# Products of activations and gates shared with GpSimd, loads by pairs and by eight, and another order at the end of a decoder layer with a PEER mixer

## The reference, cut to what matters

```python
    best, pos = lax.top_k(cand, K)
    expert_idx = jnp.take_along_axis(cand_idx, pos, axis=-1)
    gate = jax.nn.softmax(best, axis=-1)
    ...
        u = jnp.take(expert_down, idx, axis=0)
        a = jax.nn.gelu(jnp.einsum('nd,nhkd->nhk', xb, u).astype(jnp.float32), approximate=False)
        w = (gb * a).astype(xb.dtype)
        v = jnp.take(expert_up, idx, axis=0)
        return jnp.einsum('nhk,nhkd->nd', w, v)
    ...
    return rmsnorm(x, final_norm_w)
```

## Time and profile before

| | us |
|---|---|
| three runs | 1594.74, 1594.9, 1597.07 |
| median | 1594.9 |
| the profiled execution, its own time | 1598.4 |
| its span, first to last instruction | 1596.2 |
| mean granted TensorE clock | 0.997 of full speed |
| busy in the span: PE, DVE, ACT, POOL | 1568.7, 1167.0, 665.1, 977.4 |
| first instruction of block 1 of the second product | at 1084.51 |

### The profile page before, as it was taken

How to read it: one execution, slowest core, us unless ns; L and a number is a source line. 1 busy time by engine, 2 the same in 40 slices (tenths; PEclk the granted TensorE clock), 3 DMA queues, 4 the chain that set the end, 5 groups by cost and what they waited for, 6 DMA issues and landing times.

```text
span 1596.2 us, 26546 instructions
## 1 busy us (share of the span) xinstructions
PE 1568.7 (98%) x9939; PEld 1481.5 (93%) x9939; DVE 1167.0 (73%) x2248; ACT 665.1 (42%) x991; POOL 977.4 (61%) x563
## 2 busy tenths in 40 slices
PE   8999999999999999999999999999999999999997
PEld 6888888888989999999999999999999999999997
DVE  4155361342479999999999973348999999998996
ACT  5352442542434444444444443333343333333334
POOL 4463376523235899887777778875566465675632
PEclk9999999999999999999999999999999999999998
DMA  4232243313423999989999999969999999999991
GB/s 185 93 102 70 70 155 93 112 61 106 158 80 120 293 355 345 327 291 314 372 391 408 394 413 391 348 212 381 402 400 402 400 402 392 400 402 384 402 373 74
DMA packets 158768, 441.80 MB, mean 277 GB/s; under 512 B 16208, under 2 KB 66384, under 8 KB 158544
## 3 DMA queue, kind: packets, MB, share of 16 engines
q1 hardware_dynamic: 88656, 228.88, 40.6%
q0 software_dynamic: 46080, 167.79, 27.6%
q10 hardware_dynamic: 23936, 43.85, 7.2%
HBM read 396.65 MB, written 43.25 MB: 276 GB/s over the span
## 4 chain that ended last, share of the span: by engine, by line
PE 63%; DMA 15%; DVE 9%; issue 6%; ACT 2%; POOL 2%; SPq 1%; ACTq 0%; DVEq 0%
PE psum L1512 18%; PE psum L1513 18%; PE psum L1514 18%; DMA arena<-up_in 7%; DMA arena<-hid_dram 5%; PE psum L1799 4%; DVE kept L1401 3%; DVE arena L1415 2%; POOL w_low L460 2%; DVE wgt_low L1426 1%; DMA gate_dram<-arena 1%; PE psum L1748 1%; PE psum L1776 1%; DMA kept<-up_in,arena 1%; SPq L371 1%
## 5 line engine op out<-in xcount | busy, mean ns | idle before, releaser
L460 POOL TENSOR_TENSOR w_low<-kept,w_high 128x1024 fp32r<-128x1024 f32 x212 | 520.0, 2456 | 310.9 <-ACT w_high L589 309.1
L1512 PE MATMUL psum<-hT_high,w_high 128*128 128x352 f32 (+2 forms) x1408 | 484.6, 344 | 4.1 <-POOL w_low L460 3.4
L1514 PE MATMUL psum<-hT_high,w_low 128*128 128x352 f32 (+2 forms) x1408 | 476.7, 339 | 0.0
L1513 PE MATMUL psum<-hT_low,w_high 128*128 128x352 f32 (+2 forms) x1408 | 476.7, 339 | 0.0
L1512 PE MATMUL psum<-wgt_high,up_high 128*128 128x352 f32 x1016 | 329.7, 324 | 4.5 <-DVE wgt_low L1426 4.5
L1514 PE MATMUL psum<-wgt_high,up_low 128*128 128x352 f32 x1016 | 328.0, 323 | 0.0
L1513 PE MATMUL psum<-wgt_low,up_high 128*128 128x352 f32 x1016 | 327.8, 323 | 0.0
L1512 PEld LDWEIGHTS psum<-hT_high,w_high 128*128 128x128 f32 x1408 | 264.8, 188 | 18.6 <-POOL w_low L460 2.6
L589 ACT ACTIVATE w_high<-kept 128x1024 fp32r<-128x1024 f32 x212 | 223.5, 1056 | 134.1 <-PE psum L1514 90.8
L1514 PEld LDWEIGHTS psum<-hT_high,w_low 128*128 128x128 f32 x1408 | 264.7, 188 | 12.7
L1513 PEld LDWEIGHTS psum<-hT_low,w_high 128*128 128x128 f32 x1408 | 265.0, 188 | 12.0 <-issue 0.5
(11 more groups left out here) (277 smaller groups left out, 2047.9 us busy)
## 6 DMA issues: line engine op xcount, KB each, us to landing
kept<-down_in SPq DMA_DIRECT2D x128, 512.0 KB, 6.8
arena<-up_in SPq DMA_DIRECT2D x128, 512.0 KB, 13.8
kept<-front_w SPq DMA_DIRECT2D x92, 512.0 KB, 3.6
gate_dram<-arena ACTq DMA_DIRECT2D x40, 512.0 KB, 9.3
arena<-hid_dram SPq DMA_DIRECT2D x112, 176.0 KB, 12.8
kept<-gate_dram SPq DMA_DIRECT2D x24, 640.0 KB, 16.5
hid_dram<-arena ACTq DMA_DIRECT2D x56, 176.0 KB, 6.8
hid_dram<-kept ACTq DMA_DIRECT2D x56, 176.0 KB
```

The costliest lines, as they stand in the source:

```text
L460: nc.gpsimd.tensor_tensor(lower, ring[:, p % RING, :], high.bitcast(F32), ALU.subtract).then_inc(low_ready, 1)
L1512: nc.tensor.matmul(out, lhs[0], rhs[0], start=first, stop=False)
L1513: nc.tensor.matmul(out, lhs[0], rhs[1], start=False, stop=False)
L1514: return nc.tensor.matmul(out, lhs[1], rhs[0], start=False, stop=last)
```

## The change

- Activations go out and come in by pairs of blocks (352 KB): two pair buffers out (`PAIRS_OUT`), four in (`PAIRS_IN`, so eight blocks). The pair of blocks u, u + 1 is asked for when block u - 7 is weighed; the wait for DVE in SP's queue is there for every second block only.
- Gates are stored and loaded by groups of eight blocks (1280 KB), two buffers; a load of gates has 10 KB in a row for each partition, a piece of a store two rows of 2 KB. `PIECES_AT` stores a chunk's pieces by step 5 instead of step 6. The first load of gates no longer waits for the last dot.
- The 32-column product moves from DVE to POOL (`weigh_near`), with a semaphore `near_ready` that ACT's `weight_high` and SP's `load_hid` wait for. In POOL's program it stands among the gathers.
- At the end: sums of squares in parts of 512, 256 and 256 columns, tiles 0 and 1 on ACT and tile 2 on DVE; the last 256 columns of the product with the gain on DVE; the scaling and the stores in halves; PE turns bank o - 1 back behind bank o.
- Some buffers move.

```diff
-GT = 4
+GT = 8
+GROUPS = NK // GT
 PIECES = 8
-PIECES_AT = (1, 1, 1, 1, 1, 1, 2, 0)
+PIECES_AT = (2, 1, 1, 1, 2, 1, 0, 0)
...
-HIDS = 4
+PAIRS_OUT, PAIRS_IN = 2, 4
...
-        gates = [at(kb, FAR * GT * CH, FAR, GT * CH) for kb in (116, 45, 50, 55)]
-        hidr = at(60, 4 * DN, 4, DN)
+        gates = [at(kb, FAR * GT * CH, FAR, GT * CH) for kb in (192, 45)]
+        hidr = at(60, 2 * PAIRS_IN * DE, 2 * PAIRS_IN, DE)
...
-            def load_gates(i, s):
-
-                sp.dma_start(gates[s], gate_dram[:, :, bass.ds(i * CH, GT * CH)]).then_inc(ld_gate[s], 16)
-
-            def load_hid(i, s):
-                sp.dma_start(hidr[:, s, 0:DE], hid_dram[bass.ds(i, 1)].rearrange("b p n -> (b p) n")).then_inc(ld_hid[s], 16)
+            def load_gates(g, s):
+
+                sp.dma_start(gates[s], gate_dram[:, bass.ds(g, 1)].rearrange("p g c n -> p (g c) n")).then_inc(ld_gate[s], 16)
+
+            def load_hid(j, s):
+                sp.dma_start(hidr[:, 2 * s:2 * s + 2, :].rearrange("p a n -> p (a n)"),
+                             hid_dram[bass.ds(j, 1)].rearrange("b p n -> (b p) n")).then_inc(ld_hid[s], 16)
...
-                    sp.wait_ge(dot_done, ROWS)
-                    load_gates(block_of(0), 0)
+                    load_gates(SPILL // GT, 0)
...
-            def next_block(u, i, s, quad=True):
-
-                sp.wait_ge(w_raw, u * 2 - 6)
-                load_hid(i, s % 4)
+                if u % GT == GT // 2:
+                    sp.wait_ge(w_raw, u + GT // 2 - GT)
+                    load_gates((u + GT // 2 - KEEP) // GT, (u // GT + 1) % 2)
+
+            def next_block(u, i, pair, group, s, quad=True):
+
+                if s % 2 == 0:
+                    sp.wait_ge(w_raw, u - 6)
+                    sp.wait_ge(near_ready, u - 6)
+                    load_hid(pair, s // 2 % PAIRS_IN)
                 sp.wait_ge(up_done, u + 1 - RING_U)
                 load_up(i, s % RING_U)
-                if s % 4 == 0 and quad:
-                    load_gates(i + GT, (s // 4 + 1) % 4)
+                if s % GT == GT // 2 and quad:
+                    sp.wait_ge(w_raw, u - GT // 2)
+                    load_gates(group, (s // GT + 1) % 2)
...
+            def weigh_near(u):
+                if u < KEEP:
+                    pool.wait_ge(gelu_out, SPILL + u + 3)
+                    h = hid_kept[u]
+                else:
+                    pool.wait_ge(ld_hid[u // 2 % PAIRS_IN], 16 * ((u - KEEP) // 2 // PAIRS_IN + 1))
+                    h = hidr[:, u % (2 * PAIRS_IN), :]
+                if u >= 4:
+                    pool.wait_ge(w_ready, u - 3)
+                nc.gpsimd.tensor_tensor(wraw[:, u % 4, FAR * CH:DE], h[:, FAR * CH:DE], near[:, (u + SPILL) % NK, :], ALU.mult)\
+                    .then_inc(near_ready, 1)
+
             for i in range(AHEAD + 2, NK):
+                if i == NK - 3:
+                    pool.wait_ge(gate_out, 2 * STEPS + 3)
+                    weigh_near(0)
+                    weigh_near(1)
...
+            weighed = 2
             up_rows = up_in.rearrange("b p n -> (b p) n")
             for k in range(UP_ROWS):
                 if k < UP_FIRST:
                     pool.wait_ge(block_used, USED + NK - UP_FIRST + k + 1)
                 elif k == UP_FIRST:
                     pool.wait_ge(block_used, USED + NK)
+                    pool.wait_ge(dot_done, ROWS)
                 if UP_FIRST <= k < RING_C:
                     pool.wait_ge(up_done, k - UP_FIRST + 1)
                 if UP_FIRST + 2 <= k < RING_C:
-                    pool.wait_ge(w_raw, 2 * (3 if k == UP_FIRST + 2 else 6))
+                    pool.wait_ge(w_raw, 3 if k == UP_FIRST + 2 else 6)
+                    pool.wait_ge(near_ready, 3 if k == UP_FIRST + 2 else 6)
                 if k >= RING_C:
                     pool.wait_ge(sparse_added, k - RING_C + 1)
                 numbers = edge_idx[:, k:k + 1] if k < EDGE_SLOTS else idx3[:, k - EDGE_SLOTS:k - EDGE_SLOTS + 1]
                 nc.gpsimd.indirect_dma_start(rows_c[k % RING_C], None, up_rows,
                                              bass.IndirectOffsetOnAxis(numbers.bitcast(U32), 0))\
                     .then_inc(ld_c[k % RING_C], 16)
+                while weighed < min(NK, (k - RING_C) * (NK - 4) // UP_ROWS + 4 if k >= RING_C else k):
+                    weigh_near(weighed)
+                    weighed += 1
+            while weighed < NK:
+                weigh_near(weighed)
+                weighed += 1
 
             pool.wait_ge(ld_fin, 16)
-            for o in range(KC):
+            for o in range(KC - 2):
...
             def weight_high(i, s):
-                act.wait_ge(w_raw, i * 2 + 2)
+                act.wait_ge(w_raw, i + 1)
+                act.wait_ge(near_ready, i + 1)
...
-                if i >= HIDS:
-                    act.wait_ge(hid_stored[i % HIDS], 16 * (i // HIDS))
-                nc.scalar.activation(hid[i % HIDS], psum[:, 4 + i % 2, 0:DE], ACT.Gelu).then_inc(gelu_out, 1)
-                act.wait_ge(gelu_out, i + 3)
-                act.dma_start(hid_dram[i], hid[i % HIDS]).then_inc(hid_stored[i % HIDS], 16)
+                j, half = i // 2, i % 2
+                if half == 0 and j >= PAIRS_OUT:
+                    act.wait_ge(hid_stored[j % PAIRS_OUT], 16 * (j // PAIRS_OUT))
+                nc.scalar.activation(hid[j % PAIRS_OUT][:, half, :], psum[:, 4 + i % 2, 0:DE], ACT.Gelu).then_inc(gelu_out, 1)
+                if half:
+                    act.wait_ge(gelu_out, i + 3)
+                    act.dma_start(hid_dram[j], hid[j % PAIRS_OUT].rearrange("p a n -> p (a n)"))\
+                        .then_inc(hid_stored[j % PAIRS_OUT], 16)
...
-                act.dma_start(gate_dram[:, c, q * rows * CH:(q + 1) * rows * CH],
-                              stage[:, c % 2, q * rows:(q + 1) * rows, :].rearrange("p i n -> p (i n)"))\
+                act.dma_start(gate_dram[:, q * rows // GT:(q + 1) * rows // GT, c, :],
+                              stage[:, c % 2, q * rows:(q + 1) * rows, :].rearrange("p (g b) n -> p g (b n)", b=GT))\
...
-                    t = o - 5
                     act.wait_ge(x_added, 4)
-                    step.put(nc.scalar.activation(junk[:, 0:512], x[:, t, 0:512], ACT.Square, accum_out=ss[:, t:t + 1]))
                     step.end()
+                    square(o - 5, FIRST_COLS, ss)
+            act.wait_ge(x_added, 6)
+            for t in range(2):
+                step.end()
+                square(t, MORE_COLS, ss[:, NT:])
             act.wait_ge(x_added, KC)
+            for t in range(2):
+                step.end()
+                square(t, LAST_COLS, ss[:, 2 * NT:])
             step.end()
-            nc.scalar.activation(junk[:, 512:D], x[:, 0, 512:D], ACT.Square, accum_out=ss[:, NT:NT + 1]).then_inc(fin_squares, 1)
+            act.sem_inc(fin_squares, 1)
...
+            for c in (slice(0, 512), slice(512, D)):
+                step(nc.scalar.activation(fin_out[:, 1, c], fin_out[:, 1, c], ACT.Copy, scale=rs[:, 1:2]))
+                act.dma_start(out[P:2 * P, c], fin_out[:, 1, c]).then_inc(out_stored, 16)
...
-            def weigh(i, s, quad, gate_landed, landed, block, kept_hid=None):
-                dve.wait_ge(ld_gate[quad], gate_landed)
+            def weigh(i, landed, block, kept_hid=None):
+                s = i % 4
+                dve.wait_ge(ld_gate[i // GT % 2], 16 * (i // GT // 2 + 1))
                 if kept_hid is None:
-                    dve.wait_ge(ld_hid[s % 4], landed)
+                    dve.wait_ge(ld_hid[i // 2 % PAIRS_IN], 16 * ((i - KEEP) // 2 // PAIRS_IN + 1))
                 else:
                     dve.wait_ge(gelu_out, landed)
-                h = hidr[:, s % 4, :] if kept_hid is None else kept_hid
+                h = hidr[:, i % (2 * PAIRS_IN), :] if kept_hid is None else kept_hid
                 nc.vector.tensor_tensor(
-                    wraw[:, s % 4, 0:FAR * CH].rearrange("p (c n) -> p c n", n=CH),
+                    wraw[:, s, 0:FAR * CH].rearrange("p (c n) -> p c n", n=CH),
                     h[:, 0:FAR * CH].rearrange("p (c n) -> p c n", n=CH),
-                    gates[quad][:, :, (s % 4) * CH:(s % 4 + 1) * CH], ALU.mult).then_inc(w_raw, 1)
-                nc.vector.tensor_tensor(
-                    wraw[:, s % 4, FAR * CH:DE].rearrange("p (i n) -> p i n", i=1),
-                    h[:, FAR * CH:DE].rearrange("p (i n) -> p i n", i=1),
-                    near[:, block:block + 1, :], ALU.mult).then_inc(w_raw, 1)
+                    gates[i // GT % 2][:, :, i % GT * CH:(i % GT + 1) * CH], ALU.mult).then_inc(w_raw, 1)
...
-            square(2, upper, ss[:, NT + 2:NT + 3])
-            square(1, upper, ss[:, NT + 1:NT + 2])
+            square(2, LAST_COLS, ss[:, 2 * NT:])
             dve.wait_ge(fin_squares, 1)
-            nc.vector.tensor_tensor(ms[:, 0:DT], ss[:, 0:DT], ss[:, NT:NT + DT], ALU.add).then_inc(x_added, 1)
-            dve.wait_ge(kv_low, KV_PARTS + KC)
```

(62 more changed lines are left out.)

37 lines of the change are left out of this document (19 added, 18 removed).

## The result

The changed kernel takes 1648.07 us (median of 4 runs, 1647.82 to 1648.44) against 1595.26 for the kernel before: ratio 1.0329, interval [1.0317, 1.0341], slower. Its profiled execution has a span of 1646.1 us, 49.9 more than before.

| part | before | after | difference |
|---|---|---|---|
| up to block 1 | 1084.51 | 1085.93 | +1.4 |
| blocks 1 to 125 | 488.4 | 537.5 | +49.1 |
| from the edge sums to the end | 23.3 | 22.7 | -0.6 |

A forecast was written before the change was run, and what follows sets the result against it. PE was taken to bound the second stage, with DVE close behind; after the change, DVE stalled by late near products. 1594.9 + 54 (second stage) - 1.5 (first stage) - 1.5 (end) = 1646 us, range 1606 to 1690.

The forecast's parts named there:

- three classes of iterations: Second stage: near product freed by the iteration's sole row (45), first of two rows (33), or an earlier iteration's row (36).
- One sign: Second stage, changed profile: PE waits for `weight_low` in more than half of the blocks, rising from 4.5 to some 50 us.
- Stalls: DVE before `weight_low`, second stage: 1.62 us in 45 sole-row iterations, 0.7 in 33 with a first of two rows.
- DVE's base: DVE's second-stage iterations without stalls: 3.16 us each plus 1.41 per second row, 406.8 us over 114 iterations.
- The start: Start of the second stage: DVE enters some 3 us ahead of PE, used up once, so +57.4 becomes +54 us.
- First stage: Pair and gate stores in the first expert product: -1.5 us from a shorter gate-store wait, bounds -1.5 and +3.
- End: End of the program, square and addition behind the last addition go or shrink: -1.5 us, bounds -2.2 and +1.
- The near product itself: The 32-column product on POOL: about 0.25 us, fitted from POOL products of 384 and 1024 columns.
- Rival (a): Second stage: near products come in time and PE is the bound, 1583.5 us; chance 0.13.
- pairs and gates by eight: Second-stage loads: remove DVE waits behind PE's waits; bounds 0 and -8.4 us, taken as 0 since DVE is the bound.

The follow-up runs named there:

- e2: Changed kernel with POOL issuing each near product one block earlier, same instructions: 1592.50 us, ratio 0.9986 to the kernel before.
- e4: Changed kernel with the near product of blocks 4 to 123 made twice on POOL: 1684.14 us, ratio 1.0558 to the kernel before.
- e12: e2 with the near product of blocks 4 to 123 made twice on POOL: 1594.13 us, ratio 0.9996 to the kernel before.
- e6: e2 with activations stored one block at a time instead of in pairs: 1595.08 us, ratio 0.9999 to the kernel before.
- e7: Changed kernel with the near product back on DVE and activations stored one block at a time: 1593.97 us, ratio 0.9995 to the kernel before.
- e1: Changed kernel with the near product back on DVE, all else kept: 1593.60 us, ratio 0.9994 to the kernel before.
- e10: e9 with activations stored one block at a time: 1592.17 us, ratio 0.9983 to the kernel before.
- e9: e2 with gate stores' rows whole, as in the kernel before: 1592.86 us, ratio 0.9993 to the kernel before.
- e3: Changed kernel with the near product issued in front of the gather it stood behind: 1595.56 us, ratio 1.0009 to the kernel before.

## Why the prediction came out right

1646 was forecast, 1648.07 measured. The mechanism is the forecast one, step by step: near(v) behind the gather behind the row, three classes of iterations, 45 of the first in count and in fact, ACT waiting for POOL, DVE for ACT, PE for DVE. Sorted by the forecast's three classes, `weight_low` starts 1.80, 0.82 and 0.40 us (medians) behind the wide product in the 45, 33 and 36 iterations. One sign failed: PE was to wait in more than half of the blocks, and it idles before 44 of 125, for 39.7 us in all. e2 shows the place, e4 and e12 that POOL's time counts only there. That the sum is within 2 us is luck in part, as its terms were off in both directions (measured minus forecast, inside the span):

- *Stalls*: 1.40 and 0.41 instead of 1.62 and 0.7. 45 x 1.40 + 33 x 0.41 = 76.5, not 96.0: -19.5. I had taken 2.0 us for the gather between 1.68 and 2.11; it took 1.68 beside `low_up` and the wide product. The rows with 2.11 and 2.62 ran beside DVE's own 32-column product, `weight_low` and a row. The stall removes the last two, but it is not the whole reason: where the changed kernel has no stall, a gather beside `weight_low` and a row takes 1.77 (1211.29). With the first of two rows the near product (1221.08) took 0.38 us and was ready 2.64 us behind the row, not 2.75 or 3.15, since it ended 0.12 behind `low_up` and not its full 0.25. PE's waits for `weight_low` came to 30.5 us by name (39.7 with those put down to nobody) where I wrote some 50.
- *DVE's base*: 114 iterations at the measured 4.30 us are 489.8, less the stalls 413.3 instead of 406.8: +6.5. Part of it is that `low_up` beside a near product takes 1.27 instead of 1.21, and `weight_low` in some iterations 0.59 instead of 0.51.
- *The start*: I took off 3 us for DVE's lead. POOL's backlog of seven gathers made it 4.7 on the other side: +7.7. The prediction had the order of the queue right, began its count at gather 8, and took POOL to be up to date there.
- *First stage*: +1.4 instead of -1.5: +2.9, not settled, see above. *End*: -0.6 instead of -1.5: +0.9; the square and the addition that go are replaced by smaller ones that wait for ACT.

The sum is -1.5; the span grew by 49.9, forecast 51. The near product itself was well sized: 0.25 us from two rows of other sizes, 0.26 where DVE stands still. But its median over the run is 0.375 us:

```profile
L529 POOL TENSOR_TENSOR arena<-arena x128: 252/375/3134, 1063.0 to 1610.6; 128x32 f32<-128x32 f32 x128
```

Rival (a) priced the change with near products in time at 1583.5 us. Measured with them in time (e2) it is 1592.5, so that price was too low. The stage is then 482.4 us and the near product on POOL gains nothing over the one on DVE (e6 482.6, e7 481.9): both run without a gap, so DVE wasn't the bound with either. The 6 us of the second stage come with pairs and gates by eight, which the forecast priced at -8.4 if DVE were in time. They are not all owed to the loads: at TensorE's other pace (last section) the gain is 3 us (e1 485.1, e10 485.4). The medians of e1, e2, e6, e7, e9 and e10 lie 0.7 to 2.7 us under the kernel before, as the first stage gives some back, and five of the six intervals include no change.

## What to carry to other kernels

A small product given to an idle engine costs what stands ahead of it in that engine's queue, not what it lasts: write down for each such instruction which event sets the one before it free and when its consumer is due, and place it one release earlier. The same 128 instructions cost 53 us, and with one constant changed nothing that can be told from the kernel before. Doubling the suspected instruction in both places is a cheap test of whether its duration or its place is paid for. And when forecast terms are summed from steady iterations, look at the backlog with which a queue enters the stage.

## What the hardware showed that I had not expected

**The port shared by VectorE and GpSimd works against small operations of either.** A 32-column product on POOL takes 0.26 us with DVE idle, and 1.30 us when it starts 0.08 us behind a DVE row of 1.27 us: it ends 0.11 us behind it (1209.82 above). In the changed kernel 51 of the 128 near products took 0.25 to 0.27 us, 33 took 0.37 or 0.38, and 41 took 1.16 to 1.33. The Trainium skill, SBUF — State Buffer, section "SBUF: two separate sides", calls the pair of ports that the two engines share an exclusive lock, held for a whole instruction, so that the other engine blocks. The ends of these products agree with that, though less than their full 0.26 us comes behind the DVE instruction. A second one made right behind the first met the next DVE operation and took 1.23 us (e4), and one that met two DVE operations in a row took 1.57 (e3). The other way round, DVE's `weight_low`, 0.51 us elsewhere, took 2.73 beside a POOL product of 2.51:

```profile
1073.64 2.73 DVE L1468 TENSOR_TENSOR wgt_low<-arena,wgt_high 128x352 fp32r<-128x352 f32 x1
```

```profile
1073.47 2.51 POOL L465 TENSOR_TENSOR w_low<-kept,w_high 128x1024 fp32r<-128x1024 f32 x1 [2.77 <-ACT w_high L619]
```

So beside a busy DVE a POOL operation of 0.25 us is to be planned with 1.3, and at worst more.

**While it never waits, TensorE keeps one of two paces.** Without any gap, at granted clock 1.00, with the same products, eight blocks take 30.72 us in e2, e7 and e9 and 30.93 us in e1, e3 and e10, in group after group of eight from the second on: 0.1600 or 0.1611 us a product. In the slower pace not every product is slower: by the means over 60 blocks of e10 the starts are 165, 158, 159, 161, 162 and 162 ns apart, over and over, where e9 has 160 throughout. The 80 us from 1240 on, of e9 and of e10:

```profile
1240.00:1320.00 80.00, 80.00 (x502) 80.00 (x501) 76.19 (x90) 30.91 (x42) 55.08 (x49) 1.00 1.03 406
```

```profile
1240.00:1320.00 80.00, 80.00 (x498) 80.00 (x498) 76.38 (x91) 30.36 (x42) 55.03 (x49) 1.00 1.03 406
```

Over the stage that is 3 us, nearly the whole difference between e1 and e7, and as much as most of the effects looked for here. What chooses the pace isn't known from these runs; in the kernel before, groups without a wait took 30.72 us as well as 30.93.
